# HGRN scores of one chunk: 64 by 64 squares in two column strips in place of 128 by 128 squares

## What is computed

```python
q = silu(pc[..., :C_FDIM]);  fg = lb + (1.0 - lb) * sigmoid(pc[..., C_FDIM:2 * C_FDIM])
k = 1.0 - fg;  logf = log(fg);  i = pc[..., 2 * C_FDIM:2 * C_FDIM + D_MODEL]
def step(S, inp):                                  # one chunk
    qc, kc, vc, lc = inp
    b = jnp.cumsum(lc, axis=1)
    diff = b[:, :, None] - b[:, None, :]
    dec = jnp.exp(jnp.where(mask, diff, -jnp.inf))  # mask: s <= t
    att = jnp.einsum('bthk,bshk,btshk->bhts', qc, kc, dec)
    o = (jnp.einsum('bthk,bhkv->bthv', qc * jnp.exp(b), S)
         + jnp.einsum('bhts,bshv->bthv', att, vc))
    bl = b[:, -1]
    S = S * jnp.exp(bl)[..., None] + jnp.einsum('bshk,bshv->bhkv', kc * jnp.exp(bl[:, None] - b), vc)
    return S, o
```

## Time and profile before

| | us |
|---|---|
| median of 3 runs | 3548.39 (3542.87 to 3552.73) |
| the profiled execution's own time | 3544.56 |
| its span in the trace | 3542.7 |
| PE busy | 3375.7 (95%) |
| DVE busy | 1811.6 (51%) |
| POOL busy | 1030.1 (29%) |
| ACT busy | 818.1 (23%) |
| mean granted PE clock | 0.975 of full |

### The profile page before, as it was taken

One profiled execution on the slowest core, in us unless ns is written; L12 is line 12 of the kernel. 1 busy time (PEld: TensorE's weight loads), 2 busy tenths in 40 slices (PEclk: granted clock), 3 DMA queues, 4 the chain that ended last, 5 costly groups with the idle time before them and its releaser, 6 DMA issues.

```text
span 3542.7 us, 72784 instructions
## 1 busy us (share of the span) xinstructions
PE 3375.7 (95%) x29284; PEld 3225.0 (91%) x29284; DVE 1811.6 (51%) x2979; ACT 818.1 (23%) x1738; POOL 1030.1 (29%) x462
## 2 busy tenths in 40 slices
PE   8998889999999999999999989999988999999998
PEld 7998768888887899999999989999977999999998
DVE  5112774665566564444444565554465644444446
ACT  3344122333233222111111141111111211111112
POOL 3221120110113044333333332222232433333331
PEclk9998799999999999999999999999988999999999
DMA  5112530000012111111111111111111111111111
GB/s 162 67 55 90 182 115 12 23 34 15 23 34 70 44 51 49 48 42 47 47 42 47 45 51 43 49 49 55 62 62 39 54 48 41 47 44 45 47 47 67
DMA packets 80630, 194.68 MB, mean 55 GB/s; under 512 B 9160, under 2 KB 42612, under 8 KB 80280
## 3 DMA queue, kind: packets, MB, share of 16 engines
q1 hardware_dynamic: 37360, 121.39, 10.6%
q10 hardware_dynamic: 43048, 70.01, 5.8%
HBM read 163.86 MB, written 29.86 MB: 55 GB/s over the span
## 4 chain that ended last, share of the span: by engine, by line
PE 80%; DVE 5%; issue 2%; ACT 1%; DMA 1%; ACTq 1%; POOL 0%; DVEq 0%; POOLq 0%
PE psum L695 21%; PE psum L247 20%; PE psum L717 20%; PE psum L3092 3%; PE psum L2095 2%; PE psum L2112 1%; PE psum L1886 1%; PE psum L2069 1%; PE psum L2149 1%; PE psum L2011 1%; PE psum L2082 1%; DMA s_cache<-cache_a 1%; PE psum L2115 1%; DVE b_YX L2795 1%; PE psum L2175 0%
## 5 line engine op out<-in xcount | busy, mean ns | idle before, releaser
L232 POOL TENSOR_TENSOR w_hi<-w_raw,derived 128x1024 fp32r<-128x1024 f32 x215 | 426.7, 1985 | 2325.1 <-PE psum L247 1371.6
L247 PE MATMUL psum<-act_hi,w_hi 128*128 128x352 f32 x2088 | 704.4, 337 | 33.3 <-DVE act_lo L342 12.5
L247 PE MATMUL psum<-act_hi,w_lo 128*128 128x352 f32 x2088 | 679.1, 325 | 0.0
L247 PE MATMUL psum<-act_lo,w_hi 128*128 128x352 f32 x2088 | 678.5, 325 | 0.0
L234 POOL TENSOR_TENSOR w_lo<-w_raw,w_hi 128x1024 fp32r<-128x1024 f32 x215 | 536.2, 2494 | 16.9
L802 DVE TENSOR_TENSOR x<-x,psum 128x352 f32<-128x352 f32 x768 | 385.3, 520 | 235.1 <-PE psum L717 230.2
L717 PE MATMUL psum<-ff_u_hi,w_hi 128*128 128x352 f32 x1536 | 496.7, 323 | 0.0
L695 PE MATMUL psum<-act_hi,w_hi 128*128 128x352 f32 x1536 | 496.0, 323 | 0.2 <-DVE act_lo L542 0.2
L717 PE MATMUL psum<-ff_u_lo,w_hi 128*128 128x352 f32 x1536 | 495.0, 322 | 0.0
L717 PE MATMUL psum<-ff_u_hi,w_lo 128*128 128x352 f32 x1536 | 494.6, 322 | 0.0
L695 PE MATMUL psum<-act_lo,w_hi 128*128 128x352 f32 x1536 | 492.3, 321 | 0.0
(11 more groups left out here) (462 smaller groups left out, 4585.9 us busy)
## 6 DMA issues: line engine op xcount, KB each, us to landing
w_raw<-weights SPq DMA_DIRECT2D x215, 512.0 KB, 3.5
s_cache<-cache_a ACTq DMA_DIRECT2D x32, 512.0 KB, 6.4
kv<-a_qkv ACTq DMA_DIRECT2D x12, 528.0 KB, 2.7
x<-x_in ACTq DMA_DIRECT2D x8, 528.0 KB, 5.3
y<-end_y SPq DMA_DIRECT2D x12, 352.0 KB, 2.4
c_S_s<-state_c ACTq DMA_DIRECT2D x8, 512.0 KB, 3.2
s_c<-c_S_s ACTq DMA_DIRECT2D x8, 512.0 KB, 2.7
out_raw<-mix ACTq DMA_DIRECT2D x7, 528.0 KB, 7.9
```

Source lines behind the costliest of these rows:

```text
L232: pool.tensor_tensor(hi, raw, self.zeros, ALU.add).then_inc(s.sem, s.step())
L247: last = pe.matmul(out, w[:, k, :], h[:, k, cols], start=(start and k == ks[0] and m == 0), stop=(stop and k == ks[-1] and m == 2))
```

## The change

The products of the diagonal and of levels 1 to 32 are formed for each half of a block by itself: 16 squares of 64 by 64 for 8 blocks. Those of the first halves go to PSUM partitions 0 to 63 and use the first 64 columns of the array, those of the second halves go to partitions 64 to 127 and use the other 64 columns; the two alternate. All 16 fit in one PSUM bank. Level 64 forms one square of 64 by 64 for each block (keys of the first half, queries of the second), in partitions 0 to 63. On DVE the two picks of a level take the two halves of the partitions, 64 by 8 by 64 each, with masks of 64 columns; for level 64 one plain copy replaces them. The sample products and their picks stay as they are. Each group of pairs uses one bank where it used two.

```diff
--- before.py
+++ after.py
@@ -3014,9 +3014,9 @@
         uses = []
         for h in range(self.HEADS):
             act, dve = (lambda n: f"act.C.{h}.{n}"), (lambda n: f"dve.C.{h}.{n}")
-            uses += [act("vt0"), act("vt1"), act("vts"), dve("dg0"), dve("dg1"), dve("dgs")]
+            uses += [act("vt0"), act("vt1"), act("vts"), dve("dg1"), dve("dgs")]
             for m in LEVELS:
-                uses += [dve(f"m{m}_0"), dve(f"m{m}_1")] + ([dve(f"m{m}_s")] if m < DSEQ else [])
+                uses += [dve(f"m{m}_1")] + ([dve(f"m{m}_s")] if m < DSEQ else [])
                 uses += [act("so")] if m == self.READ else []
             uses += [act("kt0"), act("kt1"), act("kts"), dve("kv0"), dve("kv1"), dve("ss0"), dve("ss1"),
                      act("o0"), act("o1"), act("os")]
@@ -3085,12 +3085,16 @@
 
         def pairs(h, name, k, q, sample, after):
             pe.wait_ge(*at(after))
-            for g in range(2):
-                pe.wait_ge(*B.emptied(f"{h}.{name}{g}"))
-                for j in range(4):
-                    t = slice((4 * g + j) * P, (4 * g + j + 1) * P)
-                    last = pe.matmul(ps[:, B.of(f"{h}.{name}{g}"), j * P:(j + 1) * P], k[:, t], q[:, t], start=True, stop=True)
-                last.then_inc(s.sem, s.step(f"pe.C.{h}.{name}{g}"))
+            pe.wait_ge(*B.emptied(f"{h}.{name}1"))
+            bank = B.of(f"{h}.{name}1")
+            for b in range(NB):
+                halves = [slice(b * P + 64 * half, b * P + 64 * half + 64) for half in range(2)]
+                if name == f"m{LEVELS[-1]}_":
+                    last = pe.matmul(ps[0:64, bank, 64 * b:64 * b + 64], k[:, halves[0]], q[:, halves[1]], start=True, stop=True)
+                else:
+                    for half, t in enumerate(halves):
+                        last = pe.matmul(ps[64 * half:64 * half + 64, bank, 64 * b:64 * b + 64], k[:, t], q[:, t], start=True, stop=True)
+            last.then_inc(s.sem, s.step(f"pe.C.{h}.{name}1"))
             if sample:
                 pe.wait_ge(*B.emptied(f"{h}.{name}s"))
                 pe.matmul(ps[0:NS, B.of(f"{h}.{name}s"), 0:NS], k[:, SEQ:T], q[:, SEQ:T], start=True, stop=True)\
@@ -3279,13 +3283,17 @@
             dve.tensor_tensor(self.qp[:, :], self.q[:, :], f[:, :], ALU.mult).then_inc(s.sem, s.step(f"dve.C.{h}.qp"))
 
         def pick(h, name, mask, sample, last=None):
+            dve.wait_ge(*at(f"pe.C.{h}.{name}1"))
+            got = ps[:, B.of(f"{h}.{name}1"), :].rearrange("p (b t) -> p b t", b=NB)
+            if name == f"m{LEVELS[-1]}_":
+                dve.tensor_copy(self.att[0:64, :, 64:P], got[0:64]).then_inc(s.sem, s.step(f"dve.C.{h}.{name}1"))
+                return
             for g in range(2):
+                half = slice(64 * g, 64 * g + 64)
                 if last:
                     dve.wait_ge(*at(f"dve.C.{h}.{last}{g}"))
-                dve.wait_ge(*at(f"pe.C.{h}.{name}{g}"))
-                dve.copy_predicated(self.att[:, 4 * g:4 * g + 4], K.masks[:, mask].unsqueeze(1).broadcast_to([P, 4, P]),
-                                    ps[:, B.of(f"{h}.{name}{g}"), :].rearrange("p (j t) -> p j t", j=4))\
-                    .then_inc(s.sem, s.step(f"dve.C.{h}.{name}{g}"))
+                dve.copy_predicated(self.att[half, :, half], K.masks[half, mask, half].unsqueeze(1).broadcast_to([64, NB, 64]),
+                                    got[half]).then_inc(s.sem, s.step(f"dve.C.{h}.{name}{g}"))
             if sample:
                 dve.wait_ge(*at(f"pe.C.{h}.{name}s"))
                 if last:
```

## The result

The changed kernel takes 3510.43 us (median of 4 runs, 3504.34 to 3513.58) against 3548.27 for the kernel before on the same chip; the ratio is 0.9893 with a 95% interval of 0.9876 to 0.9910. A second series, timed later, gave 3508.18 against 3542.41, ratio 0.9909 (0.9895 to 0.9924). The prediction was 3510.

The account below looks back on a forecast made before the run. PE was taken to bound the steady heads, a DVE-PE-DVE chain the last. Seven heads at 4.85 us (34) plus 3 gave 37 us off: 3507.6 from the profiled execution, 3511.4 from the median, forecast 3510, range 3498 to 3523.

Parts of the forecast that it names:

- What a group costs: PE, each group of pairs: 1.86 us falls to 1.32 without samples, 2.22 to 1.50 with; 5.0 us saved a head.
- The lower bound: PE's saving in a head if each strip pays its first interval again in each of 8 groups: 4.1 us.
- the upper one: PE's saving in a head if entering the strips costs nothing beyond the usual 0.16 us: 5.4 us.
- That the strips run side by side: PE, in a group: each strip takes a record every 0.058 us while the other does the same.
- The five rows: Five starts of L2162 to L2165 in layer 0, where two half-array runs meet; source of the 0.058 us per strip.
- The rival in which the strips take turns: Strips do not run together in an alternating stream: group 2.25 us, 12 us dearer in all, 3560 us; chance 0.05.
- PE's wait at level 4: Steady head: PE waits about 0.15 us once a head for DVE's L3316 of level 2, with POOL's L232 in the way.
- I cost this at nothing: DVE's picks keep their number and 512 elements a partition, and level 64's copy replaces two: no added cost.
- The last head, 3 us: Last head: DVE's waits at levels 2 and 16 vanish, those at 32 and 64 shrink by 0.54 each; 3 us saved.
- the bounds of 0 to 6: Last head's saving: 0 if DVE only meets POOL earlier, 6 us if groups at low clock shorten by their full half.
- The term: The last head's saving built from DVE's waits: 0.43, 1.40, 0.54 and 0.54 us, 2.9 in all, put down as 3.
- The sum: Whole kernel: 34 us from seven steady heads plus 3 from the last, 37 us in all.

Follow-up runs that it names:

- blocks of 8: Changed kernel with each group's 8 first-half squares issued before its 8 second-half squares, instead of alternating: 3547.74 us, ratio 1.0005 to the kernel before.
- the late splitting: Changed kernel with POOL's first row splitting for a head (from head 2) held until DVE finishes level 2 two heads earlier: 3506.37 us.
- a filling: 25 full-width matmuls with unread output added in the last head, where PE otherwise waits: changed kernel 3510.52 us, kernel before 3546.22 us.

## Why the prediction was right, and where it was not

- **What a group costs: right.** 1.32 us without samples (measured 1.32), 1.50 with them (1.51). The 0.058 us per strip, the 0.25 for entering, the 0.11 for the first interval and the 0.15 for leaving, all taken from layer 0, hold here. The lower bound (4.1 us a head) and the upper one (5.4) were not needed.
- **That the strips run side by side: right, and the reason is the alternation.** The five rows were a joint of two blocks, where only about three records can overlap, so they could not bear out a whole group that runs so; that it does was shown afterwards. The rival in which the strips take turns is real: blocks of 8 are that rival, and they come out at 3547.74, no faster than before. My 3560 for it was too much, since the joint itself saves three intervals in each group.
- **PE's wait at level 4: right in place, cause and size** (0.15 predicted, 0.16 measured), shown by the late splitting. At the other levels the first pair starts 0.25 us after the last projection, so there is none. The period gained 4.75 us instead of 4.85. Seven heads gave 33.5 instead of 34.
- **"I cost this at nothing" of the picks: right in the steady head, wrong in the last.** In the period DVE's idle time takes it up; in the last head, a chain of DVE, the picks of levels 8, 16 and 32 cost 0.9 us between them.
- **The last head, 3 us: mis-sized; it gave 0.4**, and 1.0 in the second series, inside the bounds of 0 to 6. Two steps failed: the groups of levels 32 and 64 were priced at the full clock of the kernel before, with what stands behind the pairs left out of the sum, and the picks were put at nothing in a chain of DVE. By the turn of the keys it had gained 1.24 us. The term had 0.43 for level 2, 1.40 for level 16 and 0.54 each for levels 32 and 64. Level 2's wait of the earlier trace rows is gone but brings nothing, since POOL and DVE take turns until level 8 whatever PE does (there the time after the first turn is 34.13 before, 34.09 after). Level 16's 1.40 came in full. Levels 32 and 64 shrank from 0.80 to 0.47 and 0.46, 0.67 in all instead of 1.08, since they now ran at half clock (at full clock the waits are gone and a level gives 0.51). The picks took 0.9. Sum: 1.40 + 0.67 - 0.9 = 1.17. Then the turn of the keys and the state products, now at half clock, gave all of it back: 3.34 us from the turn's start to the samples' states (L3137) before, 4.56 after. Behind them 0.4 us was won again.
- **The sum.** The traces give 33.5 for seven heads and 0.4 to 1.0 for the last, so about 34 us instead of 37. That the median fell on 3510 to the microsecond is partly luck: the second series has 34 us.

The range of 3498 to 3523 held both medians.

## What to carry to other kernels

Here small squares in two column strips paid in full only where the instructions of the two strips alternated, one or two products at a time: in blocks of four they gave under half of it, in blocks of eight nothing. Where a chain is that of another engine, price a change of shape there by the distance between starts and not by the duration of one, and ask what the granted clock will be once the engine that became faster idles more. A comparison that is to leave the clock out needs the clock read over each group, not in the mean: a filling can miss a stretch, or delay the work behind it. A gain of 4 us in 3500 is read from periods in a trace, since the times can't show it.

## What the hardware did that I had not expected

- A matmul record of one column strip starts ahead of up to three earlier records of the other strip, and no more (blocks of 8: three; groups of 1.83, 1.47, 1.13 and 1.08 us for blocks of 8, 4, 2 and 1).
- Predicated copies on 64 of 128 partitions, 512 elements each, don't overlap what follows them on DVE: 0.76 us from start to start against 0.61 with 128 partitions, with durations of 0.73 in both. A tensor_tensor on 32 partitions does overlap it (1.22 us long, 1.14 to the next start).
- In one profile of the changed kernel PE stayed at half clock until past the end of the pairs, with 14.74 of 40 us busy, and level 64's group of quarter-size squares (16 records, 1.97 us) then took as long as the full-width one at full clock that it replaced (2.05 in the last head, 1.95 in the earlier trace rows). In the other profile the clock was up for level 32 and down again for level 64, so a chain of 50 us with half-idle PE varies by 0.7 us from run to run.
